# A two-group encoder step on one core: normed tokens split where they lie, another order in head 2, and later weight sums for layer 1

## The chip, the cores and the metric

The kernel runs on one core of a Trainium2 chip. Its time is the device time of one execution in microseconds (us); the median of several runs is given. A core has TensorE (PE, matmuls), VectorE (DVE), ScalarE (ACT), GpSimd (POOL) and SyncE (SP), each with its own queue of instructions executed in order, and 16 DMA engines. Waits between engines are semaphores.

## The reference

Two layers; 512 prompt tokens and 64 sample tokens with a cache of 512 positions; width 1024, 8 heads. All is float32.

```
h = rmsnorm(x);  z = h @ w_in      # B | C | xin | cq | ckv | kpe | gate_a | gate_b
y_a = B * causal_conv3(C * xin)
q   = rmsnorm(cq) @ w_uq           # per head 128 + 64 rotary
k, v from rmsnorm(ckv);  y_b = softmax(q k^T, chunk mask) v
x = x + rmsnorm((sigmoid(ga) * y_a + sigmoid(gb) * y_b) @ w_o)
x = x + rmsnorm(square(relu(rmsnorm(x) @ w1)) @ w2)
```

## The kernel before

The tokens stand as columns, in two halves of 288. A float32 operand is split into a high part (ScalarE copies it to the reduced type, tiles named `_hi`) and a low part (VectorE subtracts, `_lo`), and each product is three matmuls: high by low, low by high, high by high (lines 811 to 813). So each operand passes ScalarE, then VectorE, then TensorE. Results go to `ring`, four PSUM banks used in turn, and to `att`, the banks of the attention.

A layer is: latent projections; eight heads; the output projection with the sample's attention in between; the feed-forward in eight groups. Each head owns five blocks of `w_in` (1024 x 128 each: two gates, C, xin, B). TensorE takes a head's blocks with its projections, scores, transposes of the probabilities (`turns`, line 3527) and attention (`attended`) between them. Heads 0, 1 and 7 are plain. Heads 2 to 6 are mixed: two pairs of blocks are computed as seven half products each, by sums and differences of weights and tokens (`product(h, c, i)`, c the pair), and block B as it is (`mixed_block`). The token differences are `turn0` to `turn3`; their raw and low parts lie where `my` lies, their high parts over `x`. For this, head 0 writes the normed tokens into `x` (`normed_rows`), head 1 forms the differences from them (`head_mix`), and SP stores them to `h_kept` in three pieces (`h_store`) and loads them again in four (`h_load`) into the place of `xs_lo` when block 4 of head 1 has been read, where head 2 splits them (`normed_hi`, `normed_head_lo`). Head 2 (`FIRST_MIXED`) does its projections first, then products 0 to 6, scores, block B, turns, three products, `attended`, four products.

The weight sums of the mixed heads are made in DRAM by GpSimd's DMAs (`sums_copy`, then three additions), two per mixed head, twenty for both layers, in a pipeline from the start on. SP loads weight slots: `pos_load(q)` fills position q when the position before it in its slot has been read. Each engine's order is written out by hand: `plain_head` and `mixed_head` exist for ScalarE, VectorE and TensorE. At head 7 the sample's cache is loaded and split in the plain head (`cache_lo`), and after it the merged heads are split for the output projection (`x_hi_a`, `merged_lo`).

Feed-forward groups 2 to 7 work in pairs of blocks with seven half products (`pair`), whose sums VectorE makes from the loaded weights.

## Time and profile before

| what | value |
|---|---|
| median of 3 runs | 1727.48 us (1726.52 to 1728.12) |
| profiled execution | 1726.3 us, span 1724.5 us |
| TensorE busy | 1705.7 us, 99% of the span |
| VectorE, ScalarE, GpSimd busy | 76%, 50%, 7% |
| TensorE's granted clock | 0.997 of full speed |
| DMA | 231.54 MB, mean 134 GB/s |

The span is from the first to the last instruction of one profiled execution. Busy time of TensorE is modelled: a matmul's record is longer than the distance to the next one. "Idle before" in brackets is an engine's idle time just before an instruction, with what ended it. `xs` are the tokens that feed TensorE, `w` a weight slot, `small` the small weights of a pair of heads, `L811` line 811 of the kernel.

### The profile page before, as it was taken

What the parts mean: (1) busy time and instruction counts of PE and PEld (TensorE: products, weight loads), DVE (VectorE), ACT (ScalarE), POOL (GpSimd) and SP (SyncE); (2) the same over time, 40 slices, a digit from 0 to 9 for tenths busy, and PEclk for the clock granted to TensorE, in tenths of its full rate; (3) what the DMA queues carried; (4) which work ended last, traced back from release to release, by engine and by line L of the source; (5) the groups of instructions that cost most, each with busy time, mean ns of one, the idle gap of its engine ahead of it and who ended that gap; (6) DMA issues with size and microseconds to landing.
All of it is one profiled execution on the core that took longest, in us unless ns stands there. A gap on an engine that the chain in (4) does not pass through costs nothing.

```text
span 1724.5 us, 31894 instructions
## 1 busy us (share of the span) xinstructions
PE 1705.7 (99%) x12735; PEld 1690.9 (98%) x12735; DVE 1309.3 (76%) x2514; ACT 855.1 (50%) x1665; POOL 122.3 (7%) x163
## 2 busy tenths in 40 slices
PE   9999999999999999999999999999999999999997
PEld 9998999999999999999999999999999999999997
DVE  7788787767798786668687797777678887777665
ACT  7625454545465454436366364545435536444452
POOL 1412121212210000000001000000000000000000
PEclk9999999999999999999999999999999999999998
DMA  7899898898762232323124454343532213322231
GB/s 239 198 212 244 214 209 211 178 249 235 163 129 97 89 96 86 99 86 111 60 84 149 148 166 139 114 121 112 171 117 98 99 37 111 98 86 87 74 99 55
DMA packets 90996, 231.54 MB, mean 134 GB/s; under 512 B 9824, under 2 KB 25440, under 8 KB 90848
## 3 DMA queue, kind: packets, MB, share of 16 engines
q1 hardware_dynamic: 71968, 185.45, 33.5%
q0 software_dynamic: 17600, 41.95, 13.8%
q8 instruction: 101, 1.65, 0.4%
q10 hardware_dynamic: 1280, 2.10, 0.3%
q14 instruction: 47, 0.39, 0.1%
HBM read 214.39 MB, written 57.02 MB: 157 GB/s over the span
## 4 chain that ended last, share of the span: by engine, by line
PE 94%; DMA 2%; DVE 2%; ACT 1%; SPq 1%; issue 0%; DVEq 0%; ACTq 0%
PE ring L811 19%; PE ring L813 19%; PE ring L812 19%; PE att L811 11%; PE att L813 11%; PE att L812 11%; PE att L3527 1%; DMA cache_pe_raw<-cache_pe_in 1%; PE att L806 1%; PE att L805 1%; DMA small_raw<-small_in 1%; DMA xs_lo_raw<-h_kept 1%; PE att L818 0%; ACT rope_s L1291 0%; PE att L3343 0%
## 5 line engine op out<-in xcount | busy, mean ns | idle before, releaser
L811 PE MATMUL ring<-xs_hi,w_lo 128*128 128x288 f32 x1872 | 556.6, 297 | 4.3 <-DVE xs_lo L2744 2.2
L813 PE MATMUL ring<-xs_hi,w_hi 128*128 128x288 f32 x1872 | 551.4, 295 | 0.0
L812 PE MATMUL ring<-xs_lo,w_hi 128*128 128x288 f32 x1872 | 551.3, 294 | 0.0
L2071 DVE TENSOR_TENSOR w_lo<-w_raw,w_hi 128x1024 fp32r<-128x1024 f32 (+1 forms) x364 | 370.0, 1035 | 37.3 <-ACT w_hi L1220 27.2
L811 PEld LDWEIGHTS ring<-xs_hi,w_lo 128*128 128x128 f32 x1872 | 351.6, 188 | 7.3 <-DVE ga L2355 2.4
L812 PEld LDWEIGHTS ring<-xs_lo,w_hi 128*128 128x128 f32 x1872 | 351.7, 188 | 1.4
L813 PEld LDWEIGHTS ring<-xs_hi,w_hi 128*128 128x128 f32 x1872 | 351.5, 188 | 0.0
L813 PE MATMUL att<-f_hi,w_hi 128*128 128x288 f32 x960 | 283.2, 295 | 0.0
L812 PE MATMUL att<-f_lo,w_hi 128*128 128x288 f32 x960 | 282.9, 295 | 0.0
L811 PE MATMUL att<-f_hi,w_lo 128*128 128x288 f32 x960 | 282.6, 294 | 0.0
L811 PEld LDWEIGHTS att<-f_hi,w_lo 128*128 128x128 f32 x960 | 180.4, 188 | 0.0
L812 PEld LDWEIGHTS att<-f_lo,w_hi 128*128 128x128 f32 x960 | 180.4, 188 | 0.0
L813 PEld LDWEIGHTS att<-f_hi,w_hi 128*128 128x128 f32 x960 | 180.4, 188 | 0.0
L1212 ACT ACTIVATE w_hi<-w_raw 128x1024 fp32r<-128x1024 f32 x98 | 101.9, 1053 | 87.0 <-DMA w_raw<-blocks_in 86.8
L1220 ACT ACTIVATE w_hi<-w_raw 128x1024 fp32r<-128x1024 f32 x118 | 122.8, 1051 | 7.2 <-DMA w_raw<-blocks_in 6.5
L2923 DVE TENSOR_TENSOR my<-att,my 128x288 f32<-128x288 f32 x160 | 70.8, 451 | 67.7 <-PE att L813 67.7
L813 PE MATMUL ring<-mix_hi,w_hi 128*128 128x288 f32 x384 | 113.5, 295 | 0.0
L811 PE MATMUL ring<-mix_hi,w_lo 128*128 128x288 f32 x384 | 113.1, 295 | 0.0
L812 PE MATMUL ring<-mix_lo,w_hi 128*128 128x288 f32 x360 | 105.9, 294 | 0.0
L811 PE MATMUL ring<-turn_hi,w_lo 128*128 128x288 f32 x320 | 94.9, 296 | 0.0
L812 PE MATMUL ring<-turn_lo,w_hi 128*128 128x288 f32 x320 | 94.4, 295 | 0.0
L813 PE MATMUL ring<-turn_hi,w_hi 128*128 128x288 f32 x320 | 94.2, 295 | 0.0
(342 smaller groups left out, 3184.4 us busy)
## 6 DMA issues: line engine op xcount, KB each, us to landing
w_raw<-blocks_in SPq DMA_DIRECT2D x195, 512.0 KB, 3.7
weight_sums<-blocks_in POOLq DMA_DIRECT2D x80, 256.0 KB, 7.2
w_raw<-blocks_in SPq DMA_DIRECT2D x62, 256.0 KB, 4.6
weight_sums<-blocks_in POOLq DMA_DIRECT2D x20, 512.0 KB, 5.6
weight_sums<-weight_sums POOLq DMA_DIRECT2D x40, 256.0 KB, 7.6
w_raw<-weight_sums SPq DMA_DIRECT2D x20, 512.0 KB, 4.6
w_raw<-weight_sums SPq DMA_DIRECT2D x40, 256.0 KB, 4.4
small_raw<-small_in SPq DMA_DIRECT2D x16, 320.0 KB, 4.6
```

Of the source, the lines that this page charges most:

```text
L805: pe.matmul(out, both, keys[1], start=False, stop=False)
L806: return pe.matmul(out, both, keys[0], start=False, stop=True)
L811: pe.matmul(out, w[1], x[0], start=first, stop=False)
L812: pe.matmul(out, w[0], x[1], start=False, stop=False)
L813: return pe.matmul(out, w[0], x[0], start=False, stop=last)
L1212: act.activation(hi, raw, ACT.Copy).then_inc(pl.weights_hi, 1)
L1220: act.activation(hi, raw, ACT.Copy).then_inc(pl.weights_hi, 1)
L2071: return dve.tensor_tensor(out, a, hi.bitcast(F32), ALU.subtract)
L2923: dve.tensor_tensor(dst, src, dst, ALU.add).then_inc(pl.w2_free, 1)
L3527: last = pe.transpose(att[:, to:to + P], pl.probs[:, PO[t] + P * j:PO[t] + P * (j + 1)], ident)
```

## The change

- The normed tokens are no longer stored and loaded. Head 2 splits them from `x`, in the order of `H_ORDER`, as soon as the halves of block 4 of head 1 have been read; the high parts of the differences, which lie over `x`, are written after that (`turned_hi_of`).
- TensorE's order in head 2: products 0 and 1, projections, block B, products 2 to 5, scores, product 6, three products of the second pair, turns, three products, `attended`, the last product. ScalarE and VectorE have an order of their own for head 2 (`first_mixed_head`), and block B is copied out by ScalarE (`block_kept`) and multiplied later (`block_gated`). The weight positions of head 2 follow (`FIRST_ORDER`).
- In plain heads, the turned probabilities are copied before `next_weight(2)` and the small weights. At head 7 the cache's new columns and two of the cache differences come after the convolution's start, one of them after the weights of the output projection; the low parts of seven merged heads come before head 7's own gate.
- The ten sums of layer 1 wait until the first product of the second pair of group 2 in layer 0's feed-forward.

The core of the diff; declarations, the semaphores of `h_kept` and the unchanged body of the later mixed heads are left out:

```diff
 TURN_ORDER = (1, 2, 3, 0)
-H_ORDER = ((0, 0), (4, 0), (4, 1), (0, 1))
+H_ORDER = ((0, 0), (4, 0), (0, 1), (4, 1))
...
+FIRST_ORDER = [0, 1, 7, 8, 2, 3, 4, 5, 6]
 def r_mixed(h, i):
-    return HD0 + HEAD_BANKS[h] + i
+    return HD0 + HEAD_BANKS[h] + (FIRST_ORDER.index(i) if h == FIRST_MIXED and i < 9 else i)
+def mixed_part(h, n):
+    return FIRST_ORDER.index(n) if h == FIRST_MIXED and n < 9 else n
...
                     slot_load(L, n_head(h, j), s)
                     return
-                if j in (1, 5):
+                begun = 2 if h == FIRST_MIXED else 1
+                if j in (begun, 5):
                     sp.wait_ge(pl.sums_third, 16 * (head_sums(L, h, j // 5) + 1))
-                if j == 0:
-                    slot_load(L, n_head(h, 2), s)
+                if j < begun:
+                    slot_load(L, n_head(h, (2, 4)[j]), s)
                     return
-                if j in (1, 7):
+                if j in (begun, 7):
                     sp.dma_start(pl.slot(s)[2].rearrange("p (b k) -> p b k", b=2),
                                  pl.sums[head_sums(L, h, j // 7)][:, j // 7 * 2:j // 7 * 2 + 2, :]) \
                         .then_inc(pl.slots[s], 16)
...
-                    if (h, j) == (FIRST_MIXED - 1, 4):
-                        sp.wait_ge(pl.ring_full, full(L, r_hd(h, 4, 0)))
-                        sp.wait_ge(pl.h_stored, 48 * (L + 1))
-                        h_load(0)
-                        h_load(1)
-                        sp.wait_ge(pl.ring_full, full(L, r_hd(h, 4, 1)))
-                        h_load(2)
-                        h_load(3)
-                    elif is_mixed(h):
-                        sp.wait_ge(pl.ring_full, full(L, r_mixed(h, (1, 3, 5, 8, 9, 11, 13, 15)[j])))
+                    if is_mixed(h):
+                        last = (1, 8, 3, 5, 9, 11, 13, 15) if h == FIRST_MIXED else (1, 3, 5, 8, 9, 11, 13, 15)
+                        sp.wait_ge(pl.ring_full, full(L, r_mixed(h, last[j])))
                     else:
                         sp.wait_ge(pl.ring_full, full(L, r_hd(h, j, 1)))
                     for q in range(N_HEAD, POSITIONS + N_HEAD):
                         if pos_before(q) == HEAD_POS[h] + j:
                             pos_load(q)
-                    if h == FIRST_MIXED - 1 and j < 3:
-                        h_store(j)
...
             if L == 0:
-                sums_steps(BEFORE_KEYS, N_SUMS + 2)
+                sums_steps(BEFORE_KEYS, 2 * MIXED + 2, 0, 2 * MIXED)
+                pool.wait_ge(pl.sums_third, 16 * 2 * MIXED)
+                pool.wait_ge(pl.ring_full, full(0, r_pair(2, 1, 0)))
+                sums_copy(2 * MIXED)
+                sums_steps(2 * MIXED, N_SUMS + 2, 2 * MIXED, N_SUMS)
...
                 next_weight(1)
                 absorbed_hi(h)
                 exponents(h)
+                turned_hi(h)
                 next_weight(2)
                 small_hi(L, h + 1)
-                turned_hi(h)
                 if h == HEADS - 1:
                     eng.wait_ge(pl.cache_landed, L * 48 + 48)
                     act.activation(pl.cth[:, :, 0:PAST], pl.ctraw[:, :, 0:PAST], ACT.Copy).then_inc(pl.cache_hi, 1)
                     act.activation(pl.kch[:, 0:PAST], pl.kcraw[:, 0:PAST], ACT.Copy).then_inc(pl.cache_hi, 1)
+                eng.wait_ge(pl.ring_free, ring_freed(3, 1))
+                apart()
+                conv_begin(h)
+                if h == HEADS - 1:
                     eng.wait_ge(pl.latent_lo, L * 4 + 4)
                     eng.wait_ge(pl.key_lo, L * 2 + 2)
                     apart()
                     for to, src in ((pl.kch, pl.keh), (pl.kcl, pl.kel)):
                         ins = act.activation(to[:, PAST:NT], src[:, NP_:NT].bitcast(F32), ACT.Copy)
                     ins.then_inc(pl.cache_new, 1)
-                    eng.wait_ge(pl.nat_landed, L * 16 + 16)
-                    act.activation(pl.nah[:, :, :], pl.naraw[:, :, :], ACT.Copy).then_inc(pl.cache_hi, 1)
-                eng.wait_ge(pl.ring_free, ring_freed(3, 1))
-                apart()
-                conv_begin(h)
-                next_weight(3)
-                if h == FIRST_MIXED - 1:
-                    eng.wait_ge(pl.turn_made, 4 * (L + 1))
-                    eng.wait_ge(pl.h_stored, 48 * (L + 1))
-                    for t in TURN_ORDER:
-                        act.activation(pl.th[t][:, :, :], pl.traw[t][:, :, :], ACT.Copy).then_inc(pl.turn_hi, 1)
-                else:
+                if h != FIRST_MIXED - 1:
+                    next_weight(3)
                     next_weight(4)
             def mixed_head(h):
...
+                def block_kept(half):
+                    idx = r_mixed(h, 7 + half)
+                    eng.wait_ge(pl.ring_full, full(L, idx))
+                    eng.wait_ge(pl.ring_free, freed(L, idx - 1))
+                    act.activation(pl.ga[:, cols(half)], pl.ring[:, bank(L, idx), 0:NH], ACT.Copy) \
+                        .then_inc(pl.ring_free, 1)
                 def normed_hi(n):
                     k0, half = H_ORDER[n]
                     tile = (slice(0, P), slice(k0, k0 + 4), cols(half))
-                    eng.wait_ge(pl.h_landed[n], 16 * (L + 1))
-                    act.activation(pl.xh[tile], pl.xlraw[tile], ACT.Copy).then_inc(pl.h_hi, 1)
+                    eng.wait_ge(pl.ring_full, full(L, r_hd(h - 1, 4, half)))
+                    eng.wait_ge(pl.h_made, KC * (L + 1))
+                    act.activation(pl.xh[tile], pl.x[tile], ACT.Copy).then_inc(pl.h_hi, 1)
+                def turned_hi_of(i):
+                    t = TURN_ORDER[i]
+                    eng.wait_ge(pl.turn_made, 4 * (L + 1))
+                    eng.wait_ge(pl.h_lo, 4 * L + (3 if t < 2 else 4))
+                    act.activation(pl.th[t][:, :, :], pl.traw[t][:, :, :], ACT.Copy).then_inc(pl.turn_hi, 1)
...
                 if h == FIRST_MIXED:
+                    for n in range(4):
+                        normed_hi(n)
+                    turned_hi_of(0)
+                    snapshot(0)
                     even_projections()
+                    pos_hi(L, at + 2)
+                    block_kept(0)
                     pos_hi(L, at + 3)
-                    normed_hi(3)
-                    snapshot(0)
+                    block_kept(1)
+                    absorbed_hi(h)
+                    pos_hi(L, at + 4)
+                    pos_hi(L, at + 5)
+                    pos_hi(L, at + 6)
+                    exponents(h)
+                    snapshot(1)
+                    conv_started()
+                    pos_hi(L, at + 7)
+                    turned_hi(h)
+                    small_hi(L, h + 1)
+                    gates()
+                    return
...
             weight_hi(L, n_wo(4), SLOT_WO[4], use_wo(4))
+            eng.wait_ge(pl.nat_landed, L * 16 + 16)
+            act.activation(pl.nah[:, :, :], pl.naraw[:, :, :], ACT.Copy).then_inc(pl.cache_hi, 1)
...
-                minus(pl.xl[tile], pl.xlraw[tile], pl.xh[tile]).then_inc(pl.h_lo, 1)
+                minus(pl.xl[tile], pl.x[tile], pl.xh[tile]).then_inc(pl.h_lo, 1)
...
                     next_weight(0)
                     next_weight(1)
-                    next_weight(2)
+                next_weight(2)
                 small_lo(h + 1)
                 if h == HEADS - 1:
                     cache_lo(0, pl.ctl[:, :, 0:PAST], pl.ctraw[:, :, 0:PAST], pl.cth[:, :, 0:PAST])
-                    cache_lo(1, pl.kcl[:, 0:PAST], pl.kcraw[:, 0:PAST], pl.kch[:, 0:PAST])
-                    cache_lo(2, pl.nal[:, :, :], pl.naraw[:, :, :], pl.nah[:, :, :])
                 conv_state(h)
                 own_ring(h, 2, 1)
...
+                if h == HEADS - 1:
+                    cache_lo(1, pl.kcl[:, 0:PAST], pl.kcraw[:, 0:PAST], pl.kch[:, 0:PAST])
...
-                next_weight(3)
+                if h != FIRST_MIXED - 1:
+                    next_weight(3)
                 if h < FIRST_MIXED - 1:
                     next_weight(4)
-                elif h == FIRST_MIXED - 1:
-                    head_mix_lo(0)
-                    head_mix_lo(1)
                 attention_out(h)
                 own.wait()
+                if h == FIRST_MIXED - 1:
+                    normed_head_lo(0)
                 if h < HEADS - 1:
                     gated_out(h, 0)
+                    if h == FIRST_MIXED - 1:
+                        normed_head_lo(1)
                     gated_out(h, 1)
+                    if h == FIRST_MIXED - 1:
+                        normed_head_lo(2)
                     own_ring(h, 4, 1)
...
                 def first_difference(c):
                     src = ready(9 * c + 2)
+                    if h == FIRST_MIXED and c == 0:
+                        own_freed(8)
                     dve.tensor_tensor(pl.v1[:, :], pl.v1[:, :], src, ALU.subtract).then_inc(pl.ring_free, 1)
...
                 def even_projections():
                     rotary_sum(h, 0)
                     rotary_sum(h, 1)
+                    keys_lo(h)
                     if h == FIRST_MIXED:
-                        normed_head_lo(0)
-                    keys_lo(h)
+                        head_mix_lo(0)
+                        head_mix_lo(1)
                     rotary_lo(h)
-                    if h == FIRST_MIXED:
-                        normed_head_lo(1)
                     values_lo(h, 0)
...
+                def block_gated():
+                    dve.tensor_tensor(pl.u[:, 0:NP_], pl.ga[:, 0:NP_], pl.cv[:, 0:NP_], ALU.mult)
+                    own.step(dve.tensor_tensor(pl.u[:, NP_:NT], pl.ga[:, NP_:NT], pl.cv[:, NP_ + 2:NT + 2], ALU.mult))
+                def first_mixed_head():
+                    upper_left(0, pl.cv[:, cols(0)])
+                    normed_head_lo(3)
                     even_projections()
+                    pos_lo(L, at + 2)
                     head_mix_lo(3)
-                    upper_left(0, pl.cv[:, cols(0)])
+                    first_difference(0)
                     pos_lo(L, at + 3)
-                    first_difference(0)
-                    normed_head_lo(2)
                     second_sum(0)
-                    normed_head_lo(3)
-                else:
+                    conv_state(h)
+                    lower_left(0, pl.u[:, 2:2 + NH])
+                    conv_first_half()
+                    lower_right(0, pl.v2[:, :])
+                    pos_lo(L, at + 4)
+                    pos_lo(L, at + 5)
+                    row_maxima(h)
+                    absorbed_lo(h, pl.rest)
+                    upper_right(0, pl.cv[:, cols(1)])
+                    conv_second_half()
+                    pos_lo(L, at + 6)
+                    probabilities(h)
+                    upper_left(1, pl.gb[:, cols(0)])
+                    first_difference(1)
+                    conv_taps(h)
+                    pos_lo(L, at + 7)
+                    block_gated()
+                    second_sum(1)
+                    turned_lo(h)
+                    own.wait()
+                    lower_left(1, pl.ga[:, cols(0)])
+                    small_lo(h + 1)
+                    pos_lo(L, at + 8)
+                    lower_right(1, pl.ga[:, cols(1)])
+                    upper_right(1, pl.gb[:, cols(1)])
+                    pos_lo(L, at + 9)
...
+            for k in range(HEADS - 1):
+                merged_lo(x_part(L, X_WOA + k), k, cols(0))
             k = HEADS - 1
             gated_out(k, 0)
             own_ring(k, 4, 0)
             merge(k, slice(0, NH), pl.merged_a)
-            for k in range(HEADS - 1):
-                merged_lo(x_part(L, X_WOA + k), k, cols(0))
             weight_lo(L, n_wo(3), SLOT_WO[3])
             k = HEADS - 1
...
             weight_lo(L, n_wo(4), SLOT_WO[4])
+            cache_lo(2, pl.nal[:, :, :], pl.naraw[:, :, :], pl.nah[:, :, :])
...
-                if n % 2 == 0:
-                    eng.wait_ge(pl.weights_lo, pos_made(L, HEAD_POS[h] + n // 2))
+                part = mixed_part(h, n)
+                if part % 2 == 0 or h == FIRST_MIXED:
+                    eng.wait_ge(pl.weights_lo, pos_made(L, HEAD_POS[h] + part // 2))
                 if h == FIRST_MIXED and c == 0:
                     if i in (0, 1, 6):
-                        eng.wait_ge(pl.h_lo, 4 * L + (0, 1, 6).index(i) + 1)
+                        eng.wait_ge(pl.h_lo, 4 * L + (1 if i == 0 else 2 if i == 1 else 4))
                     else:
...
             def mixed_head(h):
                 if h == FIRST_MIXED:
+                    product(h, 0, 0)
+                    product(h, 0, 1)
                     projections(h)
+                    mixed_block(h)
+                    for i in range(2, 6):
+                        product(h, 0, i)
+                    scores(h)
+                    product(h, 0, 6)
+                    for i in range(3):
+                        product(h, 1, i)
+                    turns(h)
+                    for i in range(3, 6):
+                        product(h, 1, i)
+                    attended(h)
+                    product(h, 1, 6)
+                    return
```

## Rows read from the trace of the kernel before

**Rows 1.** The page: busy time by engine, and the busy share of DMA in 40 slices.

```profile
PE 1705.7 (99%) x12735; PEld 1690.9 (98%) x12735; DVE 1309.3 (76%) x2514; ACT 855.1 (50%) x1665; POOL 122.3 (7%) x163
...
DMA  7899898898762232323124454343532213322231
```

**Rows 2.** The waits of TensorE: engine, line, waited for; us in total, times, longest.

```profile
PE att L811 <- DVE probs_t_lo L2071: 2.4, 1, 2.4
PE ring L811 <- DVE xs_lo L2744: 2.2, 1, 2.2
...
PE att L811 <- DVE k_lo L2071: 0.7, 1, 0.7
PE ring L811 <- DVE xs_lo L2071: 0.7, 2, 0.4
PE att L811 <- DVE rx L2454: 0.6, 1, 0.6
```

**Rows 3.** Timeline of TensorE at block 4 of head 1, layers 0 and 1.

```profile
138.43 0.34 PE L811 MATMUL ring<-xs_hi,w_lo 128*128 128x288 f32 x1
...
991.01 0.34 PE L811 MATMUL ring<-xs_hi,w_lo 128*128 128x288 f32 x1
...
997.43 0.29 PE L811 MATMUL att<-cqn_hi,small_lo 128*128 128x288 f32 x1
```

**Rows 4.** The chain that ended last: start, us, what; layer 0.

```profile
122.53 10.03 DMA small_raw<-small_in
...
141.83 9.38 DMA xs_lo_raw<-h_kept
...
378.11 12.65 DMA cache_pe_raw<-cache_pe_in
```

**Rows 5.** Timeline of VectorE, heads 1 and 2 of layer 1.

```profile
986.22 2.01 DVE L2071 TENSOR_TENSOR small_lo<-small_raw,small_hi 128x1792 fp32r<-128x1792 f32 x1
988.16 0.16 DVE L2438 COPY u<-consts 128x2 f32<-128x2 f32 x1
...
993.50 0.76 DVE L2580 TENSOR_TENSOR ga<-ga,rx 128x576 f32<-128x576 f32 x1
...
997.85 0.19 DVE L2453 TENSOR_SCALAR gate_sample<-gb 128x64 f32<-128x64 f32 x1
...
1003.48 1.35 DVE L2071 TENSOR_TENSOR xs_lo<-xs_lo_raw,xs_hi 128x1152 fp32r<-128x1152 f32 x1
...
1005.46 1.87 DVE L2071 TENSOR_TENSOR q_pe<-rope_t,q_pe 64x288 fp32r<-64x288 f32 x4
```

**Rows 6.** Timeline of ScalarE, heads 1 and 2 of layer 1.

```profile
981.12 1.70 ACT L1228 ACTIVATE small_hi<-small_raw 128x1792 fp32r<-128x1792 f32 x1 [0.20 <-DMA small_raw<-small_in]
...
991.73 4.32 ACT L1576 ACTIVATE turn_hi<-turn_raw 128x1152 fp32r<-128x1152 f32 x4
998.83 3.32 ACT L1291 ACTIVATE rope_s<-att 32x288 f32<-32x288 f32 x8 [2.77 <-PE att L813]
```

**Rows 7.** Timeline of VectorE and TensorE after head 2's scores, layer 0.

```profile
170.97 0.46 DVE L2404 MEMSET att<- 64x64 f32 x4
...
176.02 1.27 DVE L2429 TENSOR_SCALAR probs<-probs,ri 128x128 f32<-128x128 f32 x4
...
177.43 1.26 PE L3527 MATMUL att<-consts,probs 128*128 128x128 f32 x10
```

**Rows 8.** The sums' third additions: durations in ns, first and last start in us.

```profile
L1142 POOL DMA_DIRECT2D weight_sums<-weight_sums x20: 805/815/1132, 77.4 to 505.0; - x20
```

**Rows 9.** DMA issues, us from issue to landing: whole run, then 165 to 330 us.

```profile
w_raw<-blocks_in SPq DMA_DIRECT2D x195, 512.0 KB, 3.7
...
w_raw<-weight_sums SPq DMA_DIRECT2D x7, 512.0 KB, 7.6
```

**Rows 10.** Timeline of VectorE and TensorE at a pair's start, group 4.

```profile
667.36 1.28 DVE L2071 TENSOR_TENSOR w_lo<-w_raw,w_hi 128x512 fp32r<-128x512 f32 x2
...
671.79 0.29 PE L811 MATMUL ring<-xs_hi,w_lo 128*128 128x288 f32 x1
```

More of the change, by code:

```diff
@@ L134, in weight_loads @@
     for q in range(POSITIONS + N_HEAD):
-        two = any(is_mixed(h) and HEAD_POS[h] + 2 <= q < HEAD_POS[h] + 7 for h in range(HEADS))
+        two = any(is_mixed(h) and HEAD_POS[h] + (3 if h == FIRST_MIXED else 2) <= q < HEAD_POS[h] + 7
+                  for h in range(HEADS))
         uses[pos_slot(q)] += 2 if two else 1
@@ L2546, in plain_head @@
                 head_out(h, pl.cv[:, cols(1)], 2, 1, pl.rx2)
-                if not first:
-                    next_weight(2)
                 if h == FIRST_MIXED - 1:
@@ L2689, in mixed_head @@
                         keys_lo(h)
-                conv_state(h)
-                lower_left(0, pl.u[:, 2:2 + NH])
-                conv_first_half()
-                lower_right(0, pl.v2[:, :])
-                upper_right(0, pl.cv[:, cols(1)])
-                conv_second_half()
-                pos_lo(L, at + 4)
-                row_maxima(h)
-                absorbed_lo(h, pl.rest)
-                conv_taps(h)
-                probabilities(h)
-                src = ready(7)
-                dve.tensor_tensor(pl.u[:, 0:NH], src, pl.cv[:, 0:NH], ALU.mult).then_inc(pl.ring_free, 1)
@@ L2704, in mixed_head @@
-                pos_lo(L, at + 5)
-                src = ready(8)
-                dve.tensor_tensor(pl.u[:, NH:NP_], src[:, 0:NP_ - NH], pl.cv[:, NH:NP_], ALU.mult)
-                dve.tensor_tensor(pl.u[:, NP_:NT], src[:, NP_ - NH:NH], pl.cv[:, NP_ + 2:NT + 2], ALU.mult) \
-                    .then_inc(pl.ring_free, 1)
-                turned_lo(h)
-                pos_lo(L, at + 6)
-                small_lo(h + 1)
-                upper_left(1, pl.gb[:, cols(0)])
-                first_difference(1)
@@ new lines, in later_mixed_head @@
+                    conv_second_half()
+                    pos_lo(L, at + 4)
+                    row_maxima(h)
+                    absorbed_lo(h, pl.rest)
+                    conv_taps(h)
+                    probabilities(h)
+                    src = ready(7)
+                    dve.tensor_tensor(pl.u[:, 0:NH], src, pl.cv[:, 0:NH], ALU.mult).then_inc(pl.ring_free, 1)
+                    pos_lo(L, at + 5)
+                    src = ready(8)
+                    dve.tensor_tensor(pl.u[:, NH:NP_], src[:, 0:NP_ - NH], pl.cv[:, NH:NP_], ALU.mult)
@@ new lines, in later_mixed_head @@
+                    dve.tensor_tensor(pl.u[:, NP_:NT], src[:, NP_ - NH:NH], pl.cv[:, NP_ + 2:NT + 2], ALU.mult) \
+                        .then_inc(pl.ring_free, 1)
+                    turned_lo(h)
+                    pos_lo(L, at + 6)
+                    small_lo(h + 1)
+                    upper_left(1, pl.gb[:, cols(0)])
+                    first_difference(1)
+                    pos_lo(L, at + 7)
+                    second_sum(1)
+                    pos_lo(L, at + 8)
+                    lower_left(1, pl.ga[:, cols(0)])
@@ L2722, in mixed_head @@
+                    pos_lo(L, at + 9)
+                    lower_right(1, pl.ga[:, cols(1)])
+                    upper_right(1, pl.gb[:, cols(1)])
+                if h == FIRST_MIXED:
+                    first_mixed_head()
+                else:
+                    later_mixed_head()
                 eng.wait_ge(pl.gated, of_head(h, 2, 0))
-                own_freed(8)
+                if h != FIRST_MIXED:
+                    own_freed(8)
                 dve.scalar_tensor_tensor(out=pl.ga[:, 0:NP_], in0=pl.ga[:, 0:NP_], scalar=1.0,
```

111 lines of the change are left out of this document (52 added, 59 removed).

## The prediction

> **What bounds the kernel.** I read the page first. TensorE is busy 1705.7 us of 1724.5, at nine tenths or more in every slice but the last [rows 1]. So no other engine's work counts in itself. The change can only take away, move or add waits of TensorE. DMA is the second thing to see: eight or nine tenths busy in the first ten slices (0 to 430 us), two or three after them.
>
> Then the list of what TensorE waited for [rows 2]. Outside the start and the end its waits are six: 2.4 us for the differences of the turned probabilities, 2.2 for `xs_lo` of line 2744, 0.6 for `rx`, 0.7 for `k_lo`, and two of 0.35 for `xs_lo` of line 2071. The idle time in a row is counted from the modelled end of a matmul, 0.29 us after its start, while matmuls of this form start every 0.13 us (48 from 991.01 to 997.43, [rows 3]). So each wait costs 0.16 us more than its row: 6.7 + 6 x 0.16 = 7.6 us. That is all that this change can win by waits, 0.44% of the time.
>
> The chain of waits shows what was late [rows 4]. In layer 0 `small_raw` was 10.0 us under way and landed at 132.6; ScalarE then copied it before it copied the turned probabilities, and TensorE waited for these (2.6 us). The normed tokens then came back from memory in 9.4 us, which held VectorE's later differences (`rx`, `k_lo`, `xs_lo`: 2.2 us). At head 7 the cache took 12.7 us and stood before the convolution on ScalarE and VectorE (2.4 us). In layer 1, where DMA is quiet, only 0.5 us is left.
>
> **Head 1: order and stores.** `turned_hi` and `turned_lo` now come ahead of `next_weight(2)` and `small_hi`, so nothing late stands before them. What is then left is layer 1's case, where the load was in time: there VectorE had the turned differences behind it when it began `small_lo` at 986.2 [rows 5], and TensorE had no wait for them [rows 2]. Gain 2.6 us in layer 0, none in layer 1. Three stores and four loads of the tokens go, 4.7 MB per layer. Behind `small_hi` now waits the convolution of head 1. Block 4 of head 1 begins at 138.4 in layer 0, at 135.8 without the wait, and at 991.0 in layer 1 [rows 3], so layer 1's times are 855.2 us later. If the small weights still landed at 132.6, which is 987.8 there, then 1.7 (copy), 2.0 (difference), 5.3 (convolution and gate, from 988.2 to the end of `ga` at 994.2 less the 0.7 that it waited for TensorE) and 0.7 (`attention_out`), all by [rows 5, 6], and 1.35 for the tokens' difference end at 998.9, and TensorE asks at 997.4: a wait of 1.5 us. In layer 1 the same load was copied right when it landed, at 981.1 [rows 6], which is 125.9 in layer 0. One store of 864 KB stood right before it in SP's queue and is gone, the sums stay. I take a landing near 129, between the two, no wait, and keep 1.5 us as the bound.
>
> **Head 2, the start.** Its first two products now need the tokens' halves just after block 4. I work in layer 1, whose rows are free of late transfers. Block 4 runs from 991.0 to 997.4 [rows 3]; its first half is full at 994.4. ScalarE's copy is 1.17 us, to 995.6, VectorE's difference 1.35 [rows 5], to 997.0. VectorE is free by then: `ga` ends at 994.2, and the weight difference and the two turned differences that followed it until 997.9 come later now. TensorE asks at 997.4. The second piece: one product by the gate (0.4) and 1.3 more, 998.6; TensorE asks at 999.0. Both are in time, by 0.3 us. The third and fourth have the projections as cover; without it the fourth would cost some 4 us.
>
> **Head 2, the projections.** `attention_out` and `keys_lo` lose the 1.3 us differences ahead of them. `pv_read` is there at 995.6, the keys' differences about 1007.6 when TensorE asks at 1008.5. So the waits for `rx`, `k_lo` and `xs_lo` go in both layers, with those of the head 1 and head 7: the 7.6 us.
>
> **Head 2, what is late next.** VectorE has to do the same work, but TensorE no longer loses time in which it caught up. TensorE's order is products 0 and 1 (to 1000.6), projections (9.1, to 1009.7), block B (6.4, to 1016.1), product 2. ScalarE: rotary copies from 1002.0 to 1005.3 (3.3 for eight), one turned copy 1.07 (4.32 for four), keys 0.6 [rows 6]. From 1007.0 VectorE owes the keys' difference (0.6), two turned ones (2.5), the rotary ones (1.9), values (1.2), a turned one (1.3), queries (0.7) and `pos_lo(at + 2)` (1.14): 1016.4, seen by TensorE at 1016.6 [rows 5]. Wait 0.55 us. Product 4 needs `pos_lo(at + 3)`, which stands behind `first_difference`: product 2 is full at 1018.4, plus 0.36 plus 1.22, against 1019.8: 0.35 us more.
>
> After the scores the old order has no slack at all: in layer 0 the memsets begin at 170.97, the probabilities end at 177.29, the transposes begin at 177.43, right behind the matmul before [rows 7]. TensorE has 6.4 us between scores and transposes in both orders (a block before, four products now). But `pos_lo(at + 4)` and `(at + 5)` now both stand before `row_maxima`, and their copies start only when the absorbed query is copied: the second ends 0.65 us after the scores do. Wait 0.65. Last, `turned_lo` stands behind `conv_taps` (1.7), a weight (1.1), the block's gate (0.6) and a sum; the three products that cover it (4.8 us) are about 0.3 short. Together 1.85 us per layer, 3.7 us in both. From below this is nothing (each wait is a difference of a long sum with an error of 0.5 or so); from above, 3 us per layer, if ScalarE's chain is 1 us longer.
>
> **Head 7.** The new tail copies, `cache_lo(1)` and `cache_lo(2)` go behind the convolution or into the output projection, and seven `merged_lo` go before the gate's product. 1,792 columns take VectorE 2.0 us and ScalarE 1.7 [rows 5, 6], so the 1,024 and 512 columns of the two are some 1.7 us of differences and 1.5 of copies, by my estimate, with the tail copies besides, that no longer stand in front of the convolution; DMA also has no sums at that time. VectorE was 2.4 us late. Wait gone, 2.4 us. `cache_lo(2)` lies in VectorE's time before the first sample maximum, some 5 us of TensorE's output projection cover it, and without this cover it costs 1.2 us.
>
> **Sums.** Twenty sums take from 19 to 505 us, 22 us each [rows 8]. The ten of layer 0 keep their place and end about 320. The others start when group 2's second pair has its first product, near 584, and end some 220 us later, near 810, where layer 1 begins its key rotation on POOL after 900. Their cost is what they do to SP's weight loads: 3.7 us with quiet DMA, 7.6 beside the sums [rows 9], so up to 4 us later. In the feed-forward a pair's second load lands just as VectorE needs it; the last two of its six differences end at 668.6, the third at 666 or so, and TensorE starts the pair at 671.8 [rows 10]. The slack is near 5 us for the first product, which needs three. Cost nothing, with the cover at 4 of 5 us.
>
> The Trainium skill ("DMA: Bandwidth & Descriptors", Queues, rings and completion order) says that each DMA engine goes in turn through the queues that have work, a packet at a time. So the two queues share the engines and the sums don't wait behind the weights. That speaks against the move, and agrees with 3.7 against 7.6 us [rows 9].
>
> **Sum.** -7.6 + 3.7 = -3.9 us. The profiled execution took 1726.3 us (span 1724.5), the median of the three runs is 1727.48: 1722.4 against the first, 1723.6 against the second.
>
> **Rivals.** (a) *Head 2 doesn't wait.* The 1.85 us per layer vanish in overlaps that I count too long: -7.6, 1719.9. For it: each is below 0.7 us. Against it: VectorE has no free time from 1003 to 1017 in the old order either. (b) *The waits move and grow.* The tokens' differences miss block 4 (margin 0.3) or the small weights still land at 132.6 (1.5), and head 2 costs 3 us per layer: -7.6 + 6 + 1.5 = -0.1, 1727.4; the change does then nothing. For it: every cover named is within 0.7 us of its need. (c) *The sums delay feed-forward.* If contended loads come over 5 us later, not 4, each of some nine pairs waits for its weights; at 1 us each that is +9 - 3.9, 1732.6. For it: 7.6 is a median, so half of the loads beside sums took longer. Against it: DMA in groups 2 to 7 is two to four tenths busy without the sums [rows 1], and the 7.6 was taken at eight or nine tenths; and the first feed-forward groups ran beside sums up to 505 without a wait of TensorE [rows 1, 2, 8]. By the rule of the Trainium skill above, turns at packets would at most halve the rate of a load of 3.7 us; that is 4 us later again, not over 5, and leaves (c) at its chance.
>
> **Chances.** Forecast (1721.6 to 1725.6) 0.5, a smaller loss or rival (a) 0.17, rival (b) 0.23, rival (c) 0.1. The range goes from 1719.6, just under (a), to 1728.2, over (b); it leaves out (c) and tails, 0.2. A measurement tells 0.2%, 3.5 us, from no change: the bound is 1724.0, inside the forecast's own range. Faster: 0.36 of the forecast's 0.5, (a) 0.17, together 0.54 with a little of (b). Same: 0.14 + 0.21, 0.35. Slower: (c) and the end of (b), 0.11.
>
> **What would show it.** Right: no row for `probs_t_lo`, `rx`, `k_lo` or line 2744 in TensorE's waits; `small_hi` of head 1 by 130; short new waits, below 1 us, of head 2 for `w_lo`, the transposes and `probs_t_lo`, in both layers alike; weight loads of groups 2 to 5 nearer 6 us, with no wait of TensorE there. Wrong: a wait before product 0 or 1 of head 2 (the margin of 0.3), waits of over 1 us in the middle of head 2, or `w_lo` waits between 580 and 810 us. A result under 1721 says that head 2 hides all; one over 1725.6 that its order is tighter than I work out.

## The result, and the profile after

The changed kernel is slower: median 1728.95 us (1725.52 to 1737.59, 22 runs) against 1725.05 us (1722.92 to 1730.66, 22 runs) of the kernel before beside it, a ratio of 1.002 with a 95% interval of 1.0012 to 1.0028, or +3.5 us (+2.1 to +4.8). Forecast were 3.9 us less. The profiled execution of after is one of its longer ones: 1733.3 us, span 1731.3, the third longest of 22; what its trace shows of the loss is more than the median lost.

First the page of after: busy time, and the busy share of DMA in 40 slices of 43 us. It answers to [rows 1].

```profile
PE 1709.4 (99%) x12735; PEld 1693.4 (98%) x12735; DVE 1311.5 (76%) x2512; ACT 856.1 (49%) x1669; POOL 122.4 (7%) x163
...
DMA  7888884353321588787124234343532213322221
```

From 260 to 510 us, where before stood at six to nine tenths, after is at two to five; from 606 to 822 us it is at seven and eight. Next what TensorE waited for, which answers to [rows 2]:

```profile
PE att L817 <- DVE my L2989: 8.3, 6, 3.4
...
PE ring L817 <- ACT ga L1581: 1.4, 2, 0.7
...
PE att L3593 <- DVE probs L2454: 0.5, 2, 0.3
```

The rows for `probs_t_lo`, `rx`, `k_lo` and `xs_lo` of the old lines 2071 and 2744 are gone. In their place stands one that the kernel before does not have: six waits, 8.3 us, for additions of `my`, the feed-forward's output. `L2989` (2923 before) is the helper that adds a bank of `att` to `my`.

Following the same matmul through both traces gives the parts. One at 452.95 before is at 447.66 after: -5.3 us up to the end of layer 0's heads. One at 868.24 before is at 874.36 after: the stretch between them, with the feed-forward of layer 0, became 11.4 us longer. One at 1301.39 is at 1308.86: +1.35 in layer 1's heads. By the forecast's terms, parted by layer, it would have been -5.3 and +1.4 for the first and the last, and 0 for the middle one.

Of the 11.4 us, 9.3 are the six waits (each its row and 0.16), at 613.7, 638.6, 710.6, 736.6, 763.3 and 790.7 us; the other 2.1 are delays too short to stand in that list. It isn't the engine's own pace: outside such gaps its matmuls start every 0.1325 us in this stretch of both traces.

### The profile page after: what moved, and what is told of

It reads as the page before. It is cut to its first block, busy times and chain, and to the rows that moved or that the text cites. A ratio compares the mean times of both kernels' runs of the same rounds, so it can differ in the third digit from the quotient of the medians.

```text
span 1731.3 us, 31903 instructions
## 1 busy us (share of the span) xinstructions
PE 1709.4 (99%) x12735; PEld 1693.4 (98%) x12735; DVE 1311.5 (76%) x2512; ACT 856.1 (49%) x1669; POOL 122.4 (7%) x163
## 4 chain that ended last, share of the span: by engine, by line
PE 92%; DVE 4%; DMA 3%; issue 1%; ACT 0%; DVEq 0%; SPq 0%; ACTq 0%
PE ring L817 19%; PE ring L819 18%; PE ring L818 18%; PE att L817 11%; PE att L819 11%; PE att L818 11%; DMA w_raw<-blocks_in 3%; PE att L3593 1%; PE att L812 1%; DVE w_lo L2096 1%; PE att L811 1%; PE att L824 0%; PE att L3409 0%; PE att L825 0%; DMA x<-x_in 0%
## 5 line engine op out<-in xcount | busy, mean ns | idle before, releaser
L2989 DVE TENSOR_TENSOR my<-att,my 128x288 f32<-128x288 f32 x160 | 70.5, 452 | 55.4 <-PE att L819 55.2
```

The source lines that it names most:

```text
L2989: dve.tensor_tensor(dst, src, dst, ALU.add).then_inc(pl.w2_free, 1)
```

## Why the feed-forward waits

The DMA view of 580 to 840 us of after: busy tenths, then issues with xcount, KB each and median us to landing.

```profile
DMA  0788978967979987787888669598599646798500
...
w_raw<-blocks_in SPq DMA_DIRECT2D x42, 512.0 KB, 5.5
weight_sums<-blocks_in POOLq DMA_DIRECT2D x40, 256.0 KB, 7.0
```

The same view of before:

```profile
DMA  0047302422241243025222312430342003645000
...
w_raw<-blocks_in SPq DMA_DIRECT2D x42, 512.0 KB, 3.6
```

So a weight takes 5.5 us in place of 3.6 as a median, less than the 7.6 that I had assumed. Single ones took longer. The same loads in both traces, least, median and longest, after first:

```profile
DMA to landing us min/median/max: 3.6/5.5/9.6
DMA to landing us min/median/max: 3.4/3.6/5.1
```

The loads behind the six waits took 7.8, 8.6, 6.2, 7.9, 8.8 and 9.4 us, 2.6 to 5.8 us more than 3.6. The longest wait shows how such a load reaches TensorE. Timeline of after: ScalarE, then VectorE (in brackets the idle time before, and what ended it), then TensorE.

```profile
780.74 1.06 ACT L1870 ACTIVATE w_hi<-w_raw 128x1024 fp32r<-128x1024 f32 x1 [5.89 <-DMA w_raw<-blocks_in]
...
787.26 0.63 ACT L1876 ACTIVATE w_hi<-w_raw 128x512 fp32r<-128x512 f32 x1 [2.03 <-DMA w_raw<-blocks_in]
```

```profile
787.32 0.69 DVE L3075 TENSOR_TENSOR w_raw<-w_raw 128x512 f32<-128x512 f32 x1 [3.45 <-issue]
...
790.23 0.45 DVE L2989 TENSOR_TENSOR my<-att,my 128x288 f32<-128x288 f32 x1
```

```profile
790.73 0.40 PE L817 MATMUL att<-f_hi,w_lo 128*128 128x288 f32 x1 [3.35 <-DVE my L2989]
```

The same VectorE instructions before:

```profile
778.52 0.45 DVE L3085 TENSOR_TENSOR ft<-pair_u,ring 128x288 f32<-128x288 f32 x1 [0.27 <-PE ring L813]
778.90 0.69 DVE L3009 TENSOR_TENSOR w_raw<-w_raw 128x512 f32<-128x512 f32 x1
...
781.80 0.45 DVE L2923 TENSOR_TENSOR my<-att,my 128x288 f32<-128x288 f32 x1
```

This is `outs_and_lo`: it begins with `pair_sums`, four sums made from both weights of the *next* pair, and only behind them stand the additions of `my` that empty the four `att` banks of the *present* block. The sums wait for the next pair's second load: SP issued it at 777.87 and it took 9.4 us; ScalarE's copy and VectorE's first sum both start when it lands, 787.3. (The 3.45 us that VectorE's row puts to "issue" are the end of this wait.) TensorE began the w2 blocks at 780.86, filled four banks (1.6 us each) by 787.3 and needed the first of them emptied: that took until 790.7. In the pair of [rows 10] TensorE began these blocks at 659.1 and the first addition came at 662.6:

```profile
659.07 0.29 PE L811 MATMUL att<-f_hi,w_lo 128*128 128x288 f32 x1
```

```profile
662.59 0.45 DVE L2923 TENSOR_TENSOR my<-att,my 128x288 f32<-128x288 f32 x1
```

With 6.4 us from four banks and 0.5 for the addition a late load has, by my estimate, some 2.4 us, not 5. I had asked when the next pair's products need the weight; the bank that VectorE's queue holds behind it is asked for earlier.

A second door leads to the same place. The chain of waits of after, at the second of the six:

```profile
623.56 8.60 DMA w_raw<-blocks_in
632.21 0.94 issue
633.15 0.43 ACT ft L1844
633.96 0.44 ACT f_hi L1847
634.86 0.45 DVE ft L3151
635.31 0.60 DVE w_raw L3075
```

Here it is ScalarE that stood at the copy of the pair's first weight, with `ft` and `f_hi` behind it, which VectorE's queue needs ahead of the sums. Three of the six waits (613.7, 638.6, 763.3) came by this door, the others by VectorE's own wait for a load.

## Experiments

All ran beside the kernel before. Its median was 1726.03 us beside e1 to e4, 1726.68 beside e5 to e8, 1726.61 beside e9 to e11, 1724.51 beside e12. Executions of one kernel lie several us apart (before: 1722.9 to 1731.3 beside e1 to e4), so verdicts rest on ratios. Each kernel has one trace, of one execution; its waits show where time went, and how much only for that execution.

### e1: the sums early again, and e2: late sums alone

```diff
 # e1, from the changed kernel
-                sums_steps(BEFORE_KEYS, 2 * MIXED + 2, 0, 2 * MIXED)
-                pool.wait_ge(pl.sums_third, 16 * 2 * MIXED)
-                pool.wait_ge(pl.ring_full, full(0, r_pair(2, 1, 0)))
-                sums_copy(2 * MIXED)
-                sums_steps(2 * MIXED, N_SUMS + 2, 2 * MIXED, N_SUMS)
+                sums_steps(BEFORE_KEYS, N_SUMS + 2, 0, N_SUMS)
 # e2: the opposite edit, in the kernel before
```

> The changed kernel with the sums of layer 1 made in one row with those of layer 0 again, as before the change. Theory A (the late sums cost the time: weight loads of groups 2 to 7 come late, VectorE stands in front of them, and the banks of the w2 products are not freed): the six waits for the additions to my go, TensorE has no wait of over 0.2 us between 450 and 860 us, and the kernel is some 4 us faster than before, ratio 0.9977, about 1721. Theory B (the loss lies in head 2's order, in both layers): the ratio stays at 1.002. If the sums beside heads 1 and 2 also hurt, the small weights land later than 130 and a wait for product 0 of up to 1.5 us is seen.

> The kernel before with nothing changed but the time of layer 1's sums, which wait for group 2's second pair. Theory A: waits for the additions to my between 600 and 810 us of 6 to 11 us, against a gain at head 7 of layer 0 of at most 2.4 us by faster cache loads: 1729 to 1734, ratio 1.003 to 1.005. Theory B: the late sums are hidden, ratio 0.9985 to 1.000.

e1: 1724.65 us, ratio 0.999 (0.998 to 1.0). e2: 1730.25, ratio 1.0025 (1.0014 to 1.0036), +4.3 us (+2.4 to +6.2). e1 has no wait of TensorE over 0.2 us between 450 and 860 us, as expected, and theory B's 1.002 is excluded, but the time missed: 1721 was expected. e2 came in the expected range of times. The waits of e1:

```profile
PE ring L817 <- DVE xs_lo L2805: 2.8, 1, 2.8
```

and of e2, the five for `my` at 617 to 789 us:

```profile
PE att L811 <- DVE my L2927: 5.3, 5, 1.4
PE att L811 <- DVE probs_t_lo L2075: 2.1, 1, 2.1
```

The waits for `my` follow the late sums, with the old heads or the new. e1 has another wait in head 7 (400.75 us), the one that I had counted as removed by the order. Its chain:

```profile
376.33 15.28 DMA cache_pe_raw<-cache_pe_in
391.63 1.07 ACT cache_t_hi L1545
```

Beside sums the cache takes 15.3 us, and even the new order doesn't cover that. In e2, with the old order and no sums, head 7 has no wait: so in after the quiet DMA alone would have been enough, and the order was not put to the test.

### e3: the additions before the sums

```diff
             def outs_and_lo(g, k0, g0, p0, g1, p1):
-                pair_sums(g1, p1)
                 f_done(g0, p0, 2)
                 w2_out(g, k0)
                 f_done(g0, p0, 3)
                 w2_out(g, k0 + 1)
+                pair_sums(g1, p1)
```

> The changed kernel, late sums kept, but in outs_and_lo VectorE does the last two differences of the pair before and two additions to my first, and the sums of the next pair's weights after them. The loads come as late as before. If the loss is VectorE's order (a late load holds the additions that free TensorE's banks), TensorE gets 3.2 us more cover: the six waits of 9.3 us shrink to under 3, and the kernel takes 1721 to 1724, ratio about 0.999. If the late loads themselves are the limit (weights of the next pair not ready), the waits only move to the start of the pairs, for w_lo, and the ratio stays at 1.002.

1727.37 us, ratio 1.0005 (0.9995 to 1.0016). The row of after at 8.3 us became:

```profile
PE att L817 <- DVE my L2989: 3.6, 6, 1.8
```

The traffic is the same; only the order of VectorE's instructions differs. Against the changed kernel the ratio fell by 0.0015, some 2.6 us, and the waits from 9.3 to 4.6 us (3.6 and six times 0.16) in traces of one execution each. So about half of the cost was the first two additions' place behind the sums, and the expectation, 1721 to 1724 us with under 3 us of waits, was missed. All six waits that are left are for the third and the fourth bank, whose additions still stand behind the sums; ScalarE's door is in two of the three pairs.

### e4: the plain heads' orders alone

```diff
 # from the kernel before: turned_hi ahead of next_weight(2) and small_hi,
 # head 7's cache differences and merged_lo placed as in the change
```

> The kernel before with only the orders of the plain heads changed: the turned probabilities before the small weights, the cache parts of head 7 behind the convolution's start and into the output projection, the seven low parts first. Tokens still go through memory, head 2 has its old order, sums as before. By my sum the waits of 2.6 and 2.4 us of layer 0 go and the four of head 2 stay: 5.0 us faster if nothing moves, ratio 0.9971. The rival: VectorE or DMA is still late at head 2 and part of the 2.6 us comes back there, since TensorE now asks 2.6 us earlier for what the tokens' load delays: ratio 0.9980 to 0.9986.

1723.26 us, ratio 0.9982 (0.9971 to 0.9993), -3.1 us: what the rival expected, not the full 5.0. The `probs_t_lo` wait and head 7's are gone, and some of the gain came back in the waits behind:

```profile
PE att L811 <- DVE k_lo L2072: 1.7, 1, 1.7
...
PE att L811 <- DVE rx L2455: 1.4, 1, 1.4
```

(0.7 and 0.6 in [rows 2]): with the old head 2 the tokens from memory are late either way. Here head 7 had no wait beside the sums, its cache landing sooner than in e1 (the two loads of `cache_pe` took a median of 9.8 us against 12.3); head 7 depends on the execution.

### e5 to e8: the sums after the heads, and head 2 in another order

```diff
 # e5, from the changed kernel; e7 the same in e4
-                pool.wait_ge(pl.ring_full, full(0, r_pair(2, 1, 0)))
+                pool.wait_ge(pl.ring_full, full(0, r_hd(HEADS - 1, 4, 1)))
 # e6: e5, and in head 2 (ScalarE; VectorE)
-                    absorbed_hi(h)
                     pos_hi(L, at + 4)
                     pos_hi(L, at + 5)
+                    absorbed_hi(h)
...
-                        head_mix_lo(2)        # in even_projections
...
                     pos_lo(L, at + 2)
+                    head_mix_lo(2)
                     head_mix_lo(3)
-                    first_difference(0)
                     pos_lo(L, at + 3)
+                    first_difference(0)
...
+                    turned_lo(h)
                     block_gated()
                     second_sum(1)
-                    turned_lo(h)
 # e8: e6 and the edit of e3
```

> The changed kernel, but layer 1's ten sums start when the last block of head 7 of layer 0 has been computed (at some 440 us) in place of group 2's second pair (616 us). Theory: sums cost time only while they run beside the loads of pairs (from about 590 us on), where VectorE stands at a pair's sums and the banks wait behind it; ten sums take some 200 us, so they are through at about 640 and meet only the first one or two pairs: 2 to 3 us of feed-forward waits are left of 8.3 to 11, and head 7 of layer 0 does not wait, since no sums run beside the loads of its cache. The heads' part of the change was worth -3.9 by the forecast: 1726.0 - 3.9 + 2.5 = 1724.6, ratio 0.999. Rival: it is the sums' total traffic beside any loads of the late layer that costs, wherever they stand after the heads: 1729 to 1731, ratio 1.002.

> As the kernel with the sums after the heads, and head 2 in another order: ScalarE splits the raw weights of positions 4 and 5 before the copies of the absorbed queries; VectorE takes the low parts of position 2 before those of the third difference, both differences and position 3 before the first difference of the products, and the turned probabilities before block B's gate. Theory: the four waits of head 2 (0.85, 0.29, 0.43, 0.26 us in each layer) are each one operation standing behind another, so they go: -3.6 us against the run with the sums after the heads, about 1721.0, ratio 0.997. Rival: TensorE then waits as long for the operations that were moved back (products 2 to 5 for the differences, block B's gate or a ring bank for its gate): 0 to -1 us, 1723.6 to 1724.6.

> The kernel before with the plain heads' orders (1723.3 in its run, ratio 0.998) and the sums of layer 1 after the heads. It has neither the new order of head 2 nor the tokens split from where they lie. Theory: the sums' place costs 2 to 3 us in the feed-forward and gives back nothing in head 7, whose wait is gone already: 1725.5, ratio 0.9997. Rival: the early sums cost something in heads 1 to 7 through the load on the DMA engines: 1721 to 1722.

> As the kernel with the sums after the heads and head 2 in another order, and VectorE adds the two last banks of a pair's second product into the output before it makes the next pair's sums. Theory: what feed-forward wait is left goes down by a half or more, as it did with the late sums (11 us there to about 4): some 1719.5 to 1720.5, ratio 0.9965. Rival: where the loads are early, the additions in front only make the pair's sums late by their own 2 to 3 us, so no gain or up to 1 us lost against the same kernel without: 1721 to 1722.

| kernel | median, us | ratio (95%) |
|---|---|---|
| e5 sums after the heads | 1724.74 | 1.0001 (0.9989 to 1.0013) |
| e6 and head 2's order | 1720.36 | 0.9973 (0.9959 to 0.9986) |
| e7 e4, sums after the heads | 1724.88 | 0.9993 (0.998 to 1.0007) |
| e8 e6, additions first | 1720.19 | 0.9961 (0.9948 to 0.9975) |

In e5 the sums ended at 623 us. One wait of a pair is left, the row below, at 620 us, where the last of them run, and two before group 1's w2 blocks, at 524 and 527 us (1.8 and 0.9):

```profile
PE att L817 <- DVE my L2989: 3.6, 1, 3.6
```

After 624 us the feed-forward of e5 has none. e6 has the same three. So sums beside these loads can cost wherever they stand. They don't always: e7, whose sums ran on to 633 us, has no wait in the feed-forward, where 2 to 3 us were expected. At 495 to 530 us the eight loads took a median of 9.1 us in e5 and 8.4 in e6, which waited there, and 7.3 in e7 and 6.5 in e8, which didn't. e6 then takes away all eight waits of head 2, in both layers, and nothing moved back: -4.4 us against e5, where -3.6 was expected. e8's trace has no wait in the feed-forward at all, but one of 2.1 us at 67 us, ahead of head 0, and its median is e6's: this doesn't show the additions' order to be worth anything without late sums. e7 is not told apart from e4 (ratio 0.9993 to 0.9982, intervals overlapping). All four times are within 1 us of what was expected.

### e9 to e11: the early row with a pause, and without

```diff
 # e10: e1 and head 2 in the order of e6.  e9: e10, and in sums_steps
+                if n + 1 == 14:
+                    pool.wait_ge(pl.cache_landed, 48)
                 if n + 1 < end:
                     sums_copy(n + 1)
 # e11: e9 and the edit of e3
```

> The changed kernel with head 2 in the other order (as in the fast run of it), and all twenty sums in one row from the start, but with a pause: step 14 of the row (at some 370 us) waits until the cache of layer 0 has landed (some 392 us), after which the row goes on and should end at about 510 us. Theory: a sum costs only where it runs beside a load that is needed at once. The loads of head 7's cache then land as without sums (no wait of 3.1 us in head 7, as the run with early sums had) and the sums are through before group 1's second blocks (524 us) and the first pair (614 us), where the kernel with the sums after the heads still waited 1.3 and 2.9 us: 1720.4 - 4.2 = 1716.2, up to 1717.5; ratio 0.995. Rival: the pause only moves the late load, to the cache's natural part or the loads at 510 to 530 us: 1720 to 1721, as the kernel with the sums after the heads.

> The changed kernel with head 2 in the other order and all twenty sums in one row from the start, without a pause: against the early sums alone (1724.7) only the order of head 2 differs, against the paused kernel only the pause. Theory: head 2's four waits go in both layers, -3.6 us, and the wait of 3 us in head 7 stays: 1721.0, ratio 0.997. Rival: with the early sums the loads of head 2's weights are late themselves, and only half is won: 1722.8.

> As the paused kernel, and the additions into the output stand before the next pair's sums. Theory: no sums run beside a pair's loads here, so the order of these VectorE instructions matters little: within 0.5 us of the paused kernel. Rival: the margin of 2.4 us that a pair's late load has is used up even without the sums, and 1 us is won; or the pair's sums come late for their products, and 1 us is lost.

e9: 1720.93 us, ratio 0.9966 (0.9951 to 0.998). e10: 1720.45, 0.9962 (0.9946 to 0.9978). e11: 1721.4, 0.9964 (0.9947 to 0.9981). The expectation of e9 missed by 4 us, and its rival came. e10 came as expected, and e11 is not told apart from e9: with no sums beside the pairs the additions' order showed no gain here either. GpSimd and TensorE of e9:

```profile
380.34 0.75 POOL L1119 DMA_DIRECT2D weight_sums<-blocks_in  x1 [59.32 <-DMA cache_pe_raw<-cache_pe_in]
...
541.65 0.83 POOL L1132 DMA_DIRECT2D weight_sums<-weight_sums  x1 [5.47 <-DMA weight_sums<-weight_sums]
```

```profile
522.98 0.58 PE L818 MATMUL att<-f_hi,w_lo 128*128 128x288 f32 x1 [2.96 <-issue]
```

The pause lasted 59 us, not 22 (it began at 321 us, since the step stood 50 us earlier in the row than I had counted), head 7 lost its wait, and the sums ended at 541.6 instead of 490: from 495 to 530 us eight weights took a median of 9.6 us, against 4.2 in e10, and TensorE waited 3.1 us there. The shorter pause wasn't tried. e10's profiled execution has the shortest span of all, 1716.1 us, with one wait of 0.6 us in head 7 in place of e1's 2.8:

```profile
PE ring L817 <- DVE xs_lo L2804: 0.6, 1, 0.6
```

Against e1 its ratio is lower by 0.003, some 5 us, where 3.6 was expected.

### e12: layer 1 without sums of its own

```diff
 def head_sums(L, h, c):
-    return 2 * MIXED * L + 2 * (h - FIRST_MIXED) + c
+    return 2 * (h - FIRST_MIXED) + c
 # and the ten late sums left out
```

> The changed kernel without the ten sums of layer 1: its mixed heads load the sums of layer 0 in their place (same sizes, same instants, other values), so this part of the computation is left out and no sums run after about 290 us. It prices the late sums at their root: everything else is the changed kernel's. Theory: the heads' part is worth the -3.9 us of the forecast (-4.1 by the changed kernel's own rows), and the late sums are the whole rest: before 1726.5 - 4 = 1722.5, 6 to 7 us under the changed kernel, with no wait of the feed-forward left and none in head 7 of layer 0; ratio 0.9977. Rival: the heads' part is worth nothing net, as the early sums' ratio of 0.999 would allow: 1725 to 1726. Second rival: the feed-forward's waits come from the new order around the output projection, not from the sums, and stay: 1728 to 1729.

1722.19 us, ratio 0.9983 (0.9973 to 0.9992), -2.9 us (-4.7 to -1.4). The list of waits has no row for `my` and none for head 7; head 2's stay. The first two of the list, the start's among them:

```profile
PE ring L3425 <- DVE clear L2175: 1.5, 1, 1.5
PE ring L817 <- ACT ga L1577: 1.4, 2, 0.7
```

So both rivals fall: the heads' part is a real gain near the forecast's, and the feed-forward's waits come with the sums and not with the order around the output projection. From this to the changed kernel the ratio rises from 0.9983 to 1.002: the late sums cost 6.4 us (4 to 9, if both intervals are combined), and turned the gain into the loss.

## Why the prediction was wrong

**The step that failed** is the one on the sums: "Cost nothing, with the cover at 4 of 5 us." They cost 4.3 us alone (e2, with the 2.4 us that head 7 gained already taken off) and 6.4 in the changed kernel (e12), and 11.4 in its profiled execution. Both numbers in that sentence were wrong. The 4 came from a median, and of the wrong rows: the 7.6 of [rows 9] is for loads of the sums themselves, while four loads from `blocks_in` in the same window had a median of 6.5. In the feed-forward the median was 5.5, less than I took, but the loads that TensorE waited for took 6.2 to 9.4, up to 5.8 later than 3.6. The cover was wrong: worked out for the weights' own use by the next pair, at 671.8, not for what stands in VectorE's queue behind the instruction that waits for them, the additions that free TensorE's banks, at some 2.4 us; e3, which moves two of these additions, shows that their place matters. I had listed rival (c) with the right sign and place, at 0.1 and 1732.6, but let its threshold of 5 us carry over from that cover; of the six loads three came 5.0, 5.2 and 5.8 us later, and the others cost as well. My argument against it, that the first feed-forward groups ran beside sums without a wait, was weak: those sums ended at 505 us, and e5, e6 and e9, whose sums went on to 623, 620 and 541, do have waits at 521 to 527 us (e7 and e8 have none). Of the sums' times the end near 810 was right (814); layer 0's ended at 253 us, not 320, which changed nothing.

**Head 1, order and stores.** Right. `probs_t_lo` doesn't wait any more, and the small weights were copied at 130.03, at the forecast's 130:

```profile
130.03 1.72 ACT L1221 ACTIVATE small_hi<-small_raw 128x1792 fp32r<-128x1792 f32 x1
```

The bound of 1.5 us behind it didn't come. In e4, with the tokens still loaded, 1.8 us came back for `k_lo` and `rx`; in after, with the tokens taken from where they lie, nothing did.

**Head 2, start and projections.** Right: no wait before products 0 and 1, in spite of a margin of 0.3 us, and none in the projections.

**Head 2, what is late next.** Right in size: 0.85, 0.28, 0.42 and 0.25 us, 1.8 per layer and alike in both (1.85 forecast). The first, by VectorE and TensorE of after:

```profile
160.37 1.22 DVE L2096 TENSOR_TENSOR w_lo<-w_raw,w_hi 128x1024 fp32r<-128x1024 f32 x1
```

```profile
161.68 0.37 PE L817 MATMUL ring<-turn_hi,w_lo 128*128 128x288 f32 x1 [0.69 <-ACT ga L1581]
```

The row names `ga`, but what came last is `w_lo(at + 2)`, ending at 161.59. Moving the queued work away removed it with the three others (e6), so each was one operation in front of another, as worked out, and none was needed.

**Head 7.** The wait is gone, but not for the reason that the sum gave first. With sums beside the cache's loads it came back at 3 us in e1 and 0.7 in e10, and without them even the old order has none (e2). The quiet DMA was named beside it, as a help; e2 shows that it is enough by itself. What the order is worth is not shown: e4 had sums and no wait, but an earlier cache. This, too, is the sums' doing, on the gain side: their move is worth up to 3 us at head 7 and costs 6 to 11 in the feed-forward.

**Sum.** -3.9 without the sums' part, against -2.9 (-4.7 to -1.4) in e12: right within what can be told. Rival (a), that head 2 hides all, needs the order of e6. The Trainium skill's rule ("DMA: Bandwidth & Descriptors", Queues, rings and completion order), that queues with work take turns packet by packet, agrees with the medians, 3.6 against 5.5 us, where half the rate would be 7.2. My inference from it, that a load is then at most 4 us later, did not hold: single loads took up to 9.6 us, and e9's eight a median of 9.6 against 4.2. No run here shows the turns themselves. The rule says nothing of who waits behind a late load, and that decided here.

## What to carry to other kernels

When background traffic is moved, don't ask when the late load's own consumer needs it, but what stands behind the first instruction that waits for it, in each engine's queue, and which banks or buffers those instructions free. The smallest of those slacks is the cover; here it was some 2.4 us where the load's own was 5. And set it against the longest loads, not the median. A stall that disappears together with traffic isn't yet cured by the order changed beside it: try the one without the other.

The best kernels here, e6 and e8 to e11 (ratios 0.9961 to 0.9973, not told apart), keep the change's heads, put two weights of head 2 ahead of what isn't urgent, and let the sums run beside the first pairs of the feed-forward at most.

## What was not expected of the hardware

A median load was only 1.9 us later beside the sums (5.5 against 3.6 us, DMA mostly at six to nine tenths), but single loads of the same 512 KB took 6.2 to 9.4 us, and it is these that TensorE waited for: the median says little of the cost. A cache load of 128 KB took 15.3 us in e1; at the same place in after the median of two is 7.3.
